# Feed-forward in seven half-size block products, with weight operands prepared in 132 pieces during the other stages

## The reference

```
h = rms_norm(x); qa|ka|va|qb|kb|vb = h @ w_in          # 1024 x 2304
A: band attention, own 64-frame chunk + 8 before, QK-norm, bias by distance (8 heads of 64)
B: window attention, own chunk + 2 before, QK-norm, rotary, sinks (8 query heads, 2 key heads)
x = x + concat(A, B) @ w_out                            # 1024 x 1024
gate, up = split(rms_norm(x) @ w_gate_up)               # 1024 x 5632
y = silu(conv_b + sum_i conv_w[i] * shifted(gate, i)) * up   # causal, width 3
x = x + y @ w_down                                      # 2816 x 1024
```

## Time and profile before

| | us |
|---|---|
| median of two runs | 2732.14 (2730.96 to 2733.31) |
| the profiled execution | 2730.9 |
| its span (first to last instruction) | 2729.1 |
| project / attend / combine / ffn, from the span's start | 0 to 480 / 480 to 965 / 965 to 1196 / 1196 to 2729 |
| busy: TensorE, DVE, ACT, POOL | 2604.4, 1376.9, 887.8, 189.9 |
| mean granted TensorE clock | 0.978 |

### The profile page before, as it was taken

How to read it: one execution, slowest core, us unless ns; L and a number is a source line. 1 busy time by engine, 2 the same in 40 slices (tenths; PEclk the granted TensorE clock), 3 DMA queues, 4 the chain that set the end, 5 groups by cost and what they waited for, 6 DMA issues and landing times.

```text
span 2729.1 us, 45154 instructions
## 1 busy us (share of the span) xinstructions
PE 2604.4 (95%) x16553; PEld 2504.4 (92%) x16553; DVE 1376.9 (50%) x2973; ACT 887.8 (33%) x1696; POOL 189.9 (7%) x125
## 2 busy tenths in 40 slices
PE   6999999589999979969999999999999999999998
PEld 3888888489999979859999999999999999999998
DVE  5544444466667645565534552554355346625651
ACT  4233332476777633232212221221122222212220
POOL 0000000332322200000000002000000210000000
PEclk8999999799999989979999999999999999999999
DMA  6232231544334165562221223322122342221221
GB/s 218 86 96 79 92 94 48 123 114 102 86 86 101 46 236 180 192 238 66 73 75 55 69 92 121 123 69 79 60 69 71 105 145 65 79 68 62 69 87 64
DMA packets 175286, 271.61 MB, mean 100 GB/s; under 512 B 19138, under 2 KB 120482, under 8 KB 175074
## 3 DMA queue, kind: packets, MB, share of 16 engines
q1 hardware_dynamic: 167842, 246.13, 29.8%
q0 software_dynamic: 4848, 23.12, 2.4%
q10 hardware_dynamic: 2512, 1.26, 0.2%
HBM read 216.35 MB, written 55.69 MB: 100 GB/s over the span
## 4 chain that ended last, share of the span: by engine, by line
PE 55%; DVE 0%; DMA 0%; POOL 0%; issue 0%; ACT 0%; SPq 0%; POOLq 0%
PE ffn_z L81 55%; DVE ffn_h_lo L1646 0%; DMA ffn_acc<-h2T_scratch 0%; ACT ffn_h_hi L1592 0%; POOL yT L1537 0%; POOL gate_sample L1542 0%; DVE ffn_acc L1703 0%; POOL gate_prompt L1543 0%; SPq L1488 0%; SPq L1486 0%; POOLq L1541 0%; POOLq L1536 0%
## 5 line engine op out<-in xcount | busy, mean ns | idle before, releaser
L81 PE MATMUL ffn_z<-ffn_h_hi,ffn_w_hi 128*128 128x352 f32 x2112 | 680.6, 322 | 22.1 <-DVE ffn_w_lo L1641 21.9
L81 PE MATMUL ffn_z<-ffn_h_lo,ffn_w_hi 128*128 128x352 f32 x2112 | 680.2, 322 | 0.0
L81 PE MATMUL ffn_z<-ffn_h_hi,ffn_w_lo 128*128 128x352 f32 x2112 | 680.0, 322 | 0.0
L1583 ACT ACTIVATE ffn_w_hi<-ffn_w_raw 128x1024 fp32r<-128x1024 f32 (+1 forms) x180 | 205.6, 1142 | 716.9 <-PE ffn_z L81 715.8
L81 PEld LDWEIGHTS ffn_z<-ffn_h_hi,ffn_w_hi 128*128 128x128 f32 x2112 | 397.2, 188 | 24.2 <-DVE ffn_w_lo L1641 23.0
L81 PEld LDWEIGHTS ffn_z<-ffn_h_hi,ffn_w_lo 128*128 128x128 f32 x2112 | 397.5, 188 | 0.0
L81 PEld LDWEIGHTS ffn_z<-ffn_h_lo,ffn_w_hi 128*128 128x128 f32 x2112 | 397.5, 188 | 0.0
L81 PE MATMUL ffn_z<-ffn_y_lo,ffn_w_hi 128*128 128x352 f32 x1056 | 340.0, 322 | 0.0
L81 PE MATMUL ffn_z<-ffn_y_hi,ffn_w_hi 128*128 128x352 f32 x1056 | 339.7, 322 | 0.0
L81 PE MATMUL ffn_z<-ffn_y_hi,ffn_w_lo 128*128 128x352 f32 x1056 | 339.5, 321 | 0.0
L242 PE MATMUL project_z<-project_w_hi,project_h_hi 128*128 128x512 f32 (+3 forms) x680 | 255.3, 375 | 13.0 <-DVE project_w_lo L411 12.9
(11 more groups left out here) (149 smaller groups left out, 3790.8 us busy)
## 6 DMA issues: line engine op xcount, KB each, us to landing
ffn_w_raw<-w_gu SPq DMA_DIRECT2D x132, 512.0 KB, 3.6
ffn_w_raw<-w_dn SPq DMA_DIRECT2D x48, 704.0 KB, 4.1
combine_w_raw<-w_o SPq DMA_DIRECT2D x24, 512.0 KB, 4.9
combine_o_raw<-oT_scratch SPq DMA_DIRECT2D x12, 704.0 KB, 6.4
combine_x<-xT SPq DMA_DIRECT2D x12, 704.0 KB, 7.4
x1T_scratch<-combine_x SPq DMA_DIRECT2D x12, 704.0 KB, 7.5
ffn_acc<-x1T_scratch POOLq DMA_DIRECT2D x3, 2816.0 KB, 11.8
yT<-ffn_acc POOLq DMA_DIRECT2D x24, 352.0 KB
```

Of the source, the lines that this page charges most:

```text
L81: last = nc.tensor.matmul(out, w_parts[w](k), act_parts[a](k), start=(k == 0 and (w, a) == PASSES[0]), stop=(k == n_k - 1 and (w, a) == PA ...
L1583: nc.scalar.activation(w_hi[s][:, 0:n_k, :], w_raw[s][:, 0:n_k, :], ACT.Copy).then_inc(w_hi_ok[s], 1)
```

## The change

**ffn.** The product of [gate, up] and of [down's column pair] with h or y is done as a 2x2 block product with seven products of half size (Winograd's form) in place of eight. The blocks of the activations are: k-tiles in two halves, tokens in two halves of 352 (A11, A12, A21, A22), with sums S1 = A21 + A22, S2 = S1 - A11, S3 = A11 - A21, S4 = A12 - S2. A group is one inner tile (4 k-tiles, 12 matmuls per product) or a pair of output tiles of down (2 k-tiles, in the first part 1). Each product still has three passes. The inner width is taken in parts of 2, 4, 4, 4, 4 and 4 tiles. Results are put together in PSUM where they can be, else by ACT copies and DVE additions. The products of neighbouring groups are interleaved. All loops are written out.

```diff
+PART_SIZES = (2, 4, 4, 4, 4, 4)
+OPERANDS = ("A11", "A12", "A22", "S1", "S2", "S3", "S4")
+H_ORDER = ("A11", "S2", "S3", "A12", "S1", "A22", "S4")
+ACT_OF = {1: "A11", 2: "A12", 3: "S4", 4: "A22", 5: "S1", 6: "S2", 7: "S3"}
+    for g, it in enumerate(groups):                    # ffn_schedule
+        late = g and not groups[g - 1]["flush"]        # flush: last inner tile of a block
+        products.append((g, 1))
+        if late: products.append((g - 1, 4))
+        products.append((g, 6))
+        if late: products.append((g - 1, 3))
+        products += [(g, 7), (g, 2)]
+        products += [(g, 4), (g, 5), (g, 3)] if it["flush"] else [(g, 5)]
...
+            for c, (g, q) in enumerate(products):       # SP: six slots of 512 KB
+                if c >= R:
+                    sp.wait_ge(prod_ok, c - R + 1)
+                src = w7_gu[...] if it["kind"] == "gu" else w7_dn[...]
+                sp.dma_start(w[c % R][:, :, 0:it["nk"], :].bitcast(F32), src).then_inc(w_ld[c % R], 16)
...
+                pe.wait_ge(w_ld[c % R], 16 * (c // R + 1))   # TensorE
+                read_back(g, q)                              # waits for ACT's or DVE's reading of the bank
+                for k in range(it["nk"]):
+                    for wp, a in PASSES: matmul(bank[:, 0:SUB], w[c % R][:, wp, k, :], (hi, lo)[a][name][:, k, :])
...
+            def load_h(b, name):                        # POOL: operands of the next block, one buffer
+                pool.wait_ge(h_lo_ok, len(OPERANDS) * b + j)
+                pool.dma_start(h_raw[:], src).then_inc(h_ld, 16)
```

```diff
+class WeightSums:
+    def load(self, eng, n):                             # 256 KB, one raw buffer
+        if at: eng.wait_ge(self.plain_ok, at)
+        eng.dma_start(self.raw[:, :, :], self.w_quads[n]).then_inc(self.ld, 16)
+    def move(self, eng, n):                             # on SP
+        self.store_plain(eng, n)                        # waits for low(), plain part; 2 x 192 KB
+        if n + 1 < self.first + self.count:
+            self.load(eng, n + 1)
+        self.store_sums(eng, n)                         # waits for low(), split part; 2 x 256 KB
+    def sums(self, eng, n):                             # on POOL, 128x128 each
+        eng.wait_ge(self.ld, 16 * (at + 1))
+        tensor_tensor(t1, b12, b11, ALU.subtract); tensor_tensor(t3, b22, b12, ALU.subtract)
+        tensor_tensor(t2, b22, t1, ALU.subtract)        # after t1
+        tensor_tensor(t4, b21, t2, ALU.subtract)        # after t2
+    def high(self, eng, n):                             # on ACT (high_here: on POOL, in attend)
+        eng.wait_ge(self.ld, 16 * (at + 1))
+        activation(self.plain[:, 0], self.raw[:, 1:4, :], ACT.Copy)
+        eng.wait_ge(self.sum_ok, 4 * at + 4)
+        activation(self.split[:, 0], self.sum, ACT.Copy)
+    def low(self, eng, n):                              # on POOL: 384, then 512 elements a partition
+PREPARED = ((0, 76), (76, 108), (108, 132))
...
             for t in range(TILES):                      # project, SP; share() spreads 76 over 80 places
                 if t + 2 < TILES:
                     load_x(t + 2)
                     load_tok(t + 2)
+                move(t, 0)
+                if t:
+                    store_a(t - 1)
+                move(t, 1)
+                move(t, 2)
+                move(t, 3)
+                if t + 2 < TILES:
+                    load_cs(t + 2)
                 store_b(t)
+                move(t, 4)
                 store_v(t)
```

```diff
             for n in range(TILES):                      # attend, SP
                 sp.wait_ge(lo_ok, 2 * (n + 1))
                 load(n + 1)
+                for at in share(n, 0):
+                    prep.move(sp, at)
                 if n:
                     store(n - 1, 1)
                 sp.wait_ge(lo_b_ok, n + 1)
                 load_b(n + 1)
+                for at in share(n, 1):
+                    prep.move(sp, at)
                 store(n, 0)
...
             for n in range(1, TILES + 1):               # attend, POOL; weights: sums, high_here, low
                 split(n)
+                weights(n - 1, 0)
                 split_b(n)
+                weights(n - 1, 1)
...
             for b, i in steps:                          # combine, SP
+                if g:
+                    move(2 * g - 1)
                 if (b, i) != steps[-1]:
                     load_w(g + 1)
                 if b < LAST:
                     load_o(b + 1, i)
+                move(2 * g)
```

More of the change, by code:

```diff
@@ L153, in place, with share @@
             return (SEQ, DEC) if t == 0 else ((t - 1) * P, P)
+        def share(t, part):
+            if t == 0:
+                return ()
+            slot, slots = 5 * (t - 1) + part, 5 * (TILES - 1)
+            first, last = prep_range
+            return range(first + (last - first) * slot // slots, first + (last - first) * (slot + 1) // slots)
         block = ctx.enter_context(nc.Block())
@@ L544, in _, with attend @@
                 norm_a(t)
-def attend(nc, q_a, k_a, qk_b, v_all, ka_cache, kb_cache, va_cache, vb_cache, rel_rows, sinks, ident, oT):
+        @block.gpsimd
+        def _(pool):
+            pool.wait_ge(w_lo_ok, KP * len(PIECES))
+            for n in range(*prep_range):
+                prep.sums(pool, n)
+                prep.low(pool, n)
+def attend(nc, q_a, k_a, qk_b, v_all, ka_cache, kb_cache, va_cache, vb_cache, rel_rows, sinks, ident, oT,
+           prep_range, w_quads, w7_gu, w7_dn):
     TILES = SEQ // P
@@ L655, in run @@
         def run(eng, step, last):
[L657 to L660 removed]
+            for n in range(TILES + 1):
                 for u in range(UNITS):
@@ L663, in run, with share @@
             last()
+        prep = WeightSums(m, prep_range, w_quads, w7_gu, w7_dn, raw_cache[:, 0:4, :], raw_cache[:, 4:8, :])
+        def share(n, part):
+            if n == 0:
+                return ()
+            slot, slots = 2 * (n - 1) + part, 2 * (TILES - 1)
+            first, last = prep_range
+            return range(first + (last - first) * slot // slots, first + (last - first) * (slot + 1) // slots)
         block = ctx.enter_context(nc.Block())
@@ L761, in split_b, with weights @@
                     .then_inc(lo_b_ok, 1)
+            def weights(n, part):
+                for at in share(n, part):
+                    prep.sums(pool, at)
+                    prep.high_here(pool, at)
+                    prep.low(pool, at)
             split_b(0)
-            for n in range(1, LOOP):
+            for n in range(1, TILES + 1):
                 split(n)
+                weights(n - 1, 0)
                 split_b(n)
-            with nc.gpsimd.Fori(LOOP, TILES + 1) as n:
-                split(n)
-                split_b(n)
+                weights(n - 1, 1)
         @block.tensor
@@ L1426, in ffn @@
     H = 2
+    R = WINO_SLOTS
+    HK = KD // 2
+    T1, T2 = slice(0, SUB), slice(SUB, BLOCK)
+    groups, products = ffn_schedule()
+    at = {gq: c for c, gq in enumerate(products)}
+    NG = len(groups)
+    gu_groups = [g for g in range(NG) if groups[g]["kind"] == "gu"]
+    dn_groups = [g for g in range(NG) if groups[g]["kind"] == "dn"]
+    finals = [g for g in dn_groups if groups[g]["p"] == len(PART_SIZES) - 1]
+    Y_UNITS = sum(PART_SIZES) // 2
+    OP_AT = {name: j for j, name in enumerate(OPERANDS)}
```

914 lines of the change are left out of this document (611 added, 303 removed).

## The result

The changed kernel takes **3207.69 us** (median of two runs, 3207.34 to 3208.03) against 2732.14 before: ratio 1.174, 95% interval 1.169 to 1.179. The forecast was 2995, with a range up to 3150: the direction was right, and the loss is 1.8 times the one forecast.

The account below looks back on a forecast made before the run. TensorE was taken as the bound, with 1510.53 us of unbroken feed-forward matmuls. Terms of -99 (ffn), +122 (project), +187 (attend) and +55 (combine) gave +265 on 2730.9, predicted 2995 us, range 2750 to 3150.

Parts of the forecast that it names:

- what comes back in ffn: Feed-forward: start, last gate groups, block turns and two-tile down groups return 90 us of the 189 us matmul gain.
- Attend: Attend: tile loads wait behind pieces in SP's queue, stopping ACT 13.3 us in 14 tiles; +187, bounds +126 and +252.
- Project: Project: 76 pieces at 7.1 us each through one raw buffer stretch the tiles; +122 us, ends +38 and +228.
- Combine: Combine: 24 pieces ahead of load_w and load_o in SP's queue lengthen the loop; +55 us, ends +15 and +95.
- ffn: Feed-forward: 1188 fewer matmuls save 189 us, less what comes back; net -99 us, bounds -169 and -30.
- start: Feed-forward's beginning: first product needs a whole split quarter, the next wait for DVE sums; +7 us.
- the two turns with their last gate groups: Feed-forward block turns: operands through one h_raw buffer, +52 us; finishing each block's last gate group, 5.5 us per block.
- the three two-tile parts: Feed-forward's two-tile part: DVE owes more than a down group lasts, 1.2 us in each of 12; +15 us.
- The forecast's own bound: Feed-forward: best case of -169 us if the operand loads hide.
- Rival B: Feed-forward: weights come too slowly, at 260 GB/s rather than 297; +100 us, 3095 us in all; chance 0.08.
- C: Rival: pieces hide in attend's SP queue and project's raw-buffer loop; all +364 us go, 2631 us; chance 0.09.
- D: Rival: project's pieces hide, attend at its lower end, combine at 15; +42 us, 2773 us; chance 0.11.

Follow-up runs that it names:

- e2: Changed kernel with SP's pieces in attend moved behind the tile loads: 2968.98 us.
- e8: Changed kernel with SP's order in attend following exactly the order in which POOL works: 2942.08 us.
- e5: Changed kernel with combine's load_w and load_o put ahead of the step's piece on SP's queue: 3185.53 us.
- e9: Changed kernel with all mends (SP's order in attend and combine, two raw buffers in project, ffn's start and turns), pieces shared 64/50/18: 2800.46 us.
- e1: Changed kernel with all 132 pieces made in a stage of their own ahead of project, three buffers each: 3271.14 us.
- e4: Changed kernel with three operand buffers at ffn's block turns, ACT's first sums between its splits, constants loaded from POOL's queue: 3168.16 us.

## Why the prediction was right or wrong

Most waits were forecast at the right places; the sum failed in what it gave them. Two terms make up 162 of the 212 us: what comes back in ffn (90 forecast, 176 measured) and attend (187 forecast, 263 measured).

- **Attend**, the largest term: right in place and mechanism, too small in size. Forecast 14 x 13.3 = 187; measured 263, above the upper end of 252. ACT's 229.7 us are 14 waits of 15.3 to 18.2, 16.2 on the mean, and one of 2.3 that was there before: 14 x 16.2 = 227, 40 more than forecast. The piece was 5.0 us against 5.2; in the tile above the loads had landed 20.3 us behind unit 3 (1057.64 - 1037.35), where the forecast had 18.5 (841.6 - 823.10), of which 0.8 is landing (5.0 for 4.2), and ACT stood at its wait 2 us earlier. Six waits for load_b add 19.1 us. What is left of the 263, some 17 us, goes with the clock: 0.81 in the stage against 0.96, TensorE busy 479 us for the same 3624 instructions that took 440. Load_b and the clock were put into the upper bound only; the clock belongs into the term, since every one of the 14 stops was sure to bring it. e2 and e8 show that all of it goes together.
- **Project**: right mechanism, +158 against +122. The piece's loop was 7.0 us where forecast at 7.1, but only without a tile's own transfers between: on the mean it is 7.5, which is 30 of the missing 37 us, and ACT's waits stretched the tile to 35.4 us. The terms left out are the tile's own stores and loads in SP's queue and beside the piece's load. POOL's prices were good at 128 elements (0.46 with a gap against 0.5) and at 384 (1.0).
- **Combine**: +68 against +55, inside its bounds. The order of SP's queue explains 19 us of it (e5); more went only with fewer pieces (e9, 18 of them) or none (e1). That is not the split the forecast had, which put it all on the order.
- **ffn**: the step that failed most. 189 us of matmuls went, as worked out, but 176 came back, not 90. The matmuls need 8316 x 0.1589 = 1321 us, the stage took 1521: 199 us over, where before it was 23. Windows like the four above give: start 34 us (before 10.5, forecast 7 more), the two turns with their last gate groups 81 (forecast 52 + 11), the three two-tile parts 34 (forecast 15), the last block's end 14.5 (forecast 5.5), the tail behind the last product 8.5 (9 before), and 27 in all outside these windows (forecast 0). In the first turn ACT's splits of the operands through the one buffer follow each other at (2218.55 - 2165.88) / 5 = 10.5 us, forecast 9.3, as two kinds of loads land after 5.8 and 7.5 us at the median, forecast 5.5. That accounts for part of the turns' 18 us; the rest of it, and the 27 us, stay open. The start was priced by its arithmetic and landing alone; that ACT's written order puts seven splits ahead of the first sum, and a DMA issue of 8.0 us ahead of all, was in the diff and was not followed. Yet that order alone is worth 6 us (e4): 28 stay with the quarters' landing and the sums of DVE behind it, which the 7 us had too low. e4 gave back 34 us at the turns by buffers; what stays there is the chain of the flush at a lower clock (0.91) and waits for acc. The forecast's own bound is off here as well: with the operand loads hidden its terms give 99 + 52 = 151, not 169. (The pitch of 0.1589 divides the chain's piece by all 9504 matmuls; 21 had run before it, and with 9483 it is 0.1593, which moves no figure here by more than 4 us.)
- **Rival B** (weights too slow, 0.08): not it. The waits of TensorE for w_gu and w_dn that the profile names come to 29 us in 1521, where B had 100, with transfers at 0.80 and 268 GB/s, less than the 297 worked out since the stage ran longer. So the weights cost something, which the sum had at nothing.
- **Rivals C and D**: the pieces do not hide as written. But C's premise holds in attend with one order changed (e8): the forecast's argument against it, that POOL's split, seven issues and a landing exceed 5.16 us, spoke of the kernel's order and not of the place.
- **POOL beside DVE**: POOL's 384- and 512-element subtractions took 998 and 1262 ns alone (e1) and 1070 and 1342 in project, a first sum 453 and 513:

```profile
L191 POOL TENSOR_TENSOR project_split<-project_stage,project_split 128x512 fp32r<-128x512 f32 x76 | 102.0, 1342 | 1.3 <-ACT project_split L169 1.3
L187 POOL TENSOR_TENSOR project_plain<-project_quads,project_plain 128x384 fp32r<-128x384 f32 x76 | 81.3, 1070 | 16.0 <-ACT project_plain L165 16.0
L153 POOL TENSOR_TENSOR project_stage<-project_quads 128x128 f32<-128x128 f32 x76 | 39.0, 513 | 290.0 <-DMA project_quads<-w_quads 290.0
L154 POOL TENSOR_TENSOR project_stage<-project_quads 128x128 f32<-128x128 f32 x76 | 37.5, 493 | 0.0
```

  With the other three sums that is 0.28 us a piece. The 0.3 that went by the rule of the Trainium skill (SBUF — State Buffer, the two sides of the SBUF) agrees; at 22 us of POOL's time, of which the loop takes part, it was no large matter.

## What to carry to other kernels

Work put on an idle engine is free only if nobody's queue waits for it in order: write down, for each queue that moves its results, what stands behind that wait and when it is due. Issue transfers in the order in which their releasers finish (attend: 263 us for nothing but that). Then count capacity: past what the gaps of project and combine hold, each further piece cost its full 4 to 5 us, while the stage it was made for gained, mended, 55 us in all, 0.4 us a piece.

## What the runs showed of the hardware

- Stops cost more than their length. In attend a stop of 17 us brought the granted clock to 0.50 of full speed (1.2 GHz), and the 7 us after it still ran at 0.50. Over the stage TensorE was busy 39 us more for the same matmuls, 2.8 us a stop; beyond the waits of ACT the stage grew by some 17 us, 1.2 a stop.
- A small DMA issue behind large ones can hold an engine: the 44 KB constant load took ACT 8.01 us to issue behind four of 704 KB, and 0.68 us from POOL's queue in e4, where nothing stood before it. Each was seen once. SP's pair of stores in project, usually 1.0 us, once took 3.35.
- POOL has a large fixed share at small tiles: 128 elements a partition took 0.45 us, 384 took 1.00, 512 took 1.26 for a subtraction of two tiles, and a rounding copy of 512 took 0.61.
